# Asking for an expert's down weights one unit later, and summing the late modulation vectors as rows in two free PSUM banks

## The chip, the cores and the metric

The program runs on one core of a Trainium2 chip. Its time is the device time in microseconds (us) of one execution; the median of several executions is compared. All numbers are float32.

## The reference, cut to what matters

The block takes 512 tokens of width 1024. Six modulation vectors come from one vector `c`; then comes a mixer (a chunked state-space branch and a sliding-window attention branch, gated and merged, one output projection, a residual), and then a mixture of 64 experts, of which each token uses 6.

```python
mod = jax.nn.silu(c) @ ada_w[i] + ada_b[i]
sh1, sc1, g1, sh2, sc2, g2 = [m[:, None, :] for m in jnp.split(mod, 6, axis=-1)]
...
merged = gates[:, :, 0] * ssd_branch + gates[:, :, 1] * attn_branch
h = h + g1 * (merged @ w_out[i])
n2 = rms_norm(h, norm2_g[i]) * (1.0 + sc2) + sh2
...
for e in range(N_EXPERTS):
    hid = jax.nn.silu(n @ e_gate[e]) * (n @ e_up[e])
    out = out + (hid @ e_down[e]) * combine[:, e:e + 1]
```

An expert has a gate and an up matrix of 1024 x 256 and a down matrix of 256 x 1024, 1 MiB each, 192 MiB for all 64. `sh2`, `sc2`, `g1` and `g2` are the "late" vectors: they are first needed after the merge.

## The kernel before, in words

Each engine has its own instruction list, written out by hand, and semaphores tie the lists together. SyncE (SP) issues nearly all loads of weights, GpSimd (POOL) the indirect gathers and scatters.

**The merge.** For each of four column blocks `i` TensorE computes three products `b` (gate of branch A, gate of branch B, attention projection) in banks `4 * jj + b` of the eight PSUM banks; `jj` is 0 or 1. So banks 3 and 7 hold nothing then. ScalarE takes the sigmoid of `b` 0 and 1 (`g_sig`), VectorE multiplies and adds (`g_read`, `merged_done`). In the trace all these products stand under line 1635 (L1635): `n1T,ring` is `b` 0 and 1, `attT,ring` is `b` 2.

**The late vectors.** Before the merge VectorE has built four partial sums of 128 partitions x 1024, one for each late vector (`late_acc`, which the trace names `siluz`), and they still have to be summed over the partitions. TensorE does this after block `i == 1`, behind waits for the merge of that block (`g_sig`, `g_read`), since it uses banks 0 to 4: for `g1` and `g2` four matmuls with an all-ones matrix, which give the sum on every partition as a row (L1645), and for `sh2` and `sc2` 16 matmuls of one output column each, which give the sum as a column (L1649). VectorE adds the biases (L1140 to L1145), and TensorE waits for that (`late_read`) before block `i == 2`.

**The experts.** The work is a sequence of units. A unit is 128 gathered rows: of one expert, or 64 each of two. The first 36 units (`BEFORE`) are unrolled, in the order `FPFPFPFP` and then four times `SPSPSSP` (F and S: one expert, P: two); a loop runs the remaining units, two experts each. TensorE does for unit `v`: the gates and ups (`gate_up`, L1771), the transposes of the next unit's rows (L1759), then the downs of unit `v - 1` (`down`, L1779), then the transposes of its own hidden rows (L1786). `gate_up` releases `gu_ready`, `down` releases `ey_ready`.

There are six slots for weights (`gu_*` for gate and up, `dn_*` for down). When a unit has used its slots, SP refills them with the experts of `REFILL[un]`: it reads the experts' numbers (`expert`, L473), waits for the gates and ups of unit `un`, issues the loads of gates and ups (L459, L460), waits for the downs of unit `un`, which TensorE does only behind the gates and ups of unit `un + 1`, issues the loads of downs (L463), and goes to the next unit. All go through one queue. The loop behind the unrolled units has the same order of waits in code of its own.

Of the kernel before, what the change touches and what calls it, by code (L numbers as in the profile page):

```python
# [13 lines left out]
SEQ = 512  # L14
D = 1024
# [74 lines left out]
def hybrid_ssd_swa_moe_adaln_block(nc, a):  # L90
# [36 lines left out]
    OUTER = 6  # L127
    PARTS = [slice(0, 1), slice(1, 3), slice(3, KC)]
    NLATE = 4 * KC

    w_gate = a["exp_w_gate"][0].rearrange("e (p k) f -> e p k f", k=KC)
    w_up = a["exp_w_up"][0].rearrange("e (p k) f -> e p k f", k=KC)
# [7 lines left out]
    with ExitStack() as ctx:  # L140
# [82 lines left out]
        def flat(ap):  # L223
            return ap.rearrange("p a b -> p (a b)")
# [171 lines left out]
        def load_turns(eng):  # L396
            eng.wait_ge(ordered, TABLE)
            return eng.value_load(turns_i[0:1, 0:1], min_val=0, max_val=4) + 1

        @block.sync  # L400
        def _(sp):
# [60 lines left out]
            def load_dn(s, e):  # L462
                sp.dma_start(dn(s)[:, :, :], which(w_down, e)).then_inc(dn_in[s], 16)  # L463
# [16 lines left out]
            load_gu(FIXED + 1, ids[1])  # L480
            sp.wait_ge(sy_ready, T)
            load_dn(FIXED + 1, ids[1])
            for un in range(BEFORE):
                ids = [expert(r) for r in REFILL[un]]
                if ids:
                    sp.wait_ge(gu_ready, un + 1)
                    for r, e in zip(REFILL[un], ids):
                        load_gu(SLOT[r], e)
                    sp.wait_ge(ey_ready, un + 1)
                    for r, e in zip(REFILL[un], ids):  # L490
                        load_dn(SLOT[r], e)
            count = load_turns(sp)
            with sp.Fori(0, count) as j:
                for m in range(LAST):
# [439 lines left out]
        def _(dve):  # L934
            steps = [0]

            def chain(ins):

                steps[0] += 1
                ins.then_inc(dve_step, 1)  # L940
                dve.wait_ge(dve_step, steps[0])
# [179 lines left out]
                    late_step(m)  # L1121
            for m in range(2 * NCH, NLATE):
                late_step(m)
            for i in range(D // WB):
                for jj in range(2):
                    dve.wait_ge(b_done, 2 * i + jj + 1)
                    dve.wait_ge(g_sig, 4 * i + jj + 1)
                    dve.tensor_tensor(sg[jj], branch[2 * i + jj], sg[jj], ALU.mult).then_inc(g_ssd, 1)
                for jj in range(2):
                    dve.wait_ge(g_ready, 6 * i + 4 + jj + 1)  # L1130
                    dve.wait_ge(g_sig, 4 * i + 2 + jj + 1)
                    dve.tensor_tensor(sg[2 + jj], ps[:, 4 * jj + 2, :], sg[2 + jj], ALU.mult).then_inc(g_read, 1)
                    dve.wait_ge(g_ssd, 2 * i + jj + 1)
                    dve.wait_ge(g_read, 2 * i + jj + 1)
                    dve.tensor_tensor(mergedT[:, 2 * i + jj, :], sg[jj], sg[2 + jj], ALU.add).then_inc(merged_done, 1)  # L1135
                if i == 1:

                    dve.wait_ge(late_ready, 1)
                    dve.wait_ge(vec_in, 16 * NVEC)
                    dve.tensor_tensor(g1_row[:, :], g1_row[:, :], flat(ps[:, 0:2, :]), ALU.add)  # L1140
                    dve.tensor_tensor(g2_row[:, :], g2_row[:, :], flat(ps[:, 2:4, :]), ALU.add)
                    dve.tensor_tensor(mod2[:, 1, :], ps[:, 4, 0:8], ab[0], ALU.add)
                    chain(dve.tensor_tensor(mod2[:, 0, :], ps[:, 4, 8:16], ab[1], ALU.add))
                    chain(dve.tensor_scalar(mod2[:, 0, :], mod2[:, 0, :], 1.0, None, ALU.add))
                    dve.tensor_tensor(mod2[:, 0, :], mod2[:, 0, :], n2g, ALU.mult).then_inc(late_read, 1)  # L1145
            dve.wait_ge(late_read, 1)
            dve.wait_ge(x_in[0], 32)

            def residual(t, half):
# [246 lines left out]
        def _(pe):  # L1396
# [224 lines left out]
                    qk(c + 2)  # L1621


            pe.wait_ge(att_done, NCH)
            for i in range(D // WB):
                for b in range(3):
                    w = block_in(BLK_M + 3 * i + b)
                    src = (n1T, n1T, attT)[b]
                    for jj in range(2):
# [5 lines left out]
                            ins = pe.matmul(ps[:, 4 * jj + b, :], w[:, k, P * jj:P * jj + P], src[:, k, :],  # L1635
                                            start=(k == 0), stop=(k == KC - 1))
                        ins.then_inc(g_ready, 1)
                if i == 1:

                    pe.wait_ge(late_used, NLATE)  # L1640
                    pe.wait_ge(g_sig, 8)
                    pe.wait_ge(g_read, 4)
                    for s, bank in ((0, 0), (3, 2)):
                        for half in range(2):
                            pe.matmul(ps[:, bank + half, :], ones[:, :], late_acc[:, s, BANK * half:BANK * half + BANK],  # L1645
                                      start=True, stop=True)
                    for s in range(2):
                        for k in range(KC):
                            ins = pe.matmul(ps[:, 4, 8 * s + k:8 * s + k + 1],  # L1649
                                            late_acc[:, 1 + s, :].rearrange("p (f k) -> p k f", k=KC)[:, k, :],  # L1650
                                            ones[:, 0:1], start=True, stop=True)
                    ins.then_inc(late_ready, 1)
                    pe.wait_ge(late_read, 1)
            pe.wait_ge(g_sig, 16)
            pe.wait_ge(g_read, 8)
            pe.wait_ge(merged_done, KC)

            def out_rows(t, b):
                w = block_in(BLK_OUT + b)
# [252 lines left out]
```

## Time and profile before

| what | value |
|---|---|
| time of the kernel before, median of 3 | 1306.63 us (1306.05 to 1307.37) |
| time of the profiled execution | 1308.78 us |
| its span, from the first to the last instruction | 1307.1 us |
| TensorE (PE) busy | 1200.8 us, 92% |
| VectorE (DVE), ScalarE (ACT), GpSimd (POOL) busy | 36%, 19%, 15% |
| mean granted TensorE clock | 0.971 |
| moved by the DMA engines | 322.29 MB |

PE busy, DVE busy and so on are shares of the span. The granted clock is the share of TensorE's full 2.4 GHz clock that it was given; it has two levels, 1.00 (2.4 GHz) and 0.50 (1.2 GHz). "DMA share" is the mean busy share of the core's 16 DMA engines; since packets overlap a little it can read 1.01 or 1.02. A name such as `SPq` is the queue of instructions of an engine, in which it waits and issues transfers. In the names of the trace `_lo` and `_hi` are two parts of the six slots.

### The profile page before, as it was taken

Reading aid. Unit: us, or ns where it says so; the run is one execution under the profiler, and the core shown is the slowest. Engines: PE = TensorE matmul, PEld = TensorE weight load, DVE = VectorE, ACT = ScalarE, POOL = GpSimd, SP = SyncE. Lnnn points to the kernel's source line nnn. Section 1 sums busy time; section 2 is a strip of 40 time slices with the busy share of each in tenths; the row PEclk is TensorE's granted clock in tenths of the full one; section 3 lists DMA queues with packets and bytes.
Section 4 is the critical chain, followed back from the end, with each engine's and each line's share of the span. In section 5 each row is a group of like instructions: output and inputs, shape, how many; then the busy total and the mean of one; then the engine's idle time right before and its main releaser. Section 6 shows DMA issues by size and latency. Waiting matters only on the chain. (4 is left out here: it accounts for less than half of the span.)

```text
span 1307.1 us, 13433 instructions
## 1 busy us (share of the span) xinstructions
PE 1200.8 (92%) x4827; PEld 621.5 (48%) x4827; DVE 473.3 (36%) x986; ACT 246.0 (19%) x611; POOL 195.8 (15%) x320
## 2 busy tenths in 40 slices
PE   4999999998999999999999999989989989988866
PEld 2536864465554444448854444434434434433322
DVE  4685034665566101113765232222323222222225
ACT  2141122234441000001121121111212111111101
POOL 4000021111012000010261212212121212211100
PEclk9999999999999998999999999989989999999988
DMA  9642241213548141237157899999999999999646
GB/s 301 186 129 64 78 149 65 97 33 129 160 125 296 65 161 33 65 105 322 72 198 274 301 419 422 423 424 421 417 396 419 400 388 412 353 414 412 264 196 276
DMA packets 108106, 322.29 MB, mean 247 GB/s; under 512 B 14500, under 2 KB 67832, under 8 KB 81032
## 3 DMA queue, kind: packets, MB, share of 16 engines
q1 hardware_dynamic: 87824, 269.37, 53.8%
q0 software_dynamic: 18688, 47.30, 10.1%
q10 hardware_dynamic: 1528, 4.77, 0.9%
q8 instruction: 39, 0.64, 0.2%
q14 instruction: 27, 0.22, 0.0%
HBM read 314.49 MB, written 26.82 MB: 261 GB/s over the span
## 5 line engine op out<-in xcount | busy, mean ns | idle before, releaser
L1771 PE MATMUL ps<-gu_hi,xsT 128*64 128x512 f32 (+1 forms) x704 | 247.5, 622 | 27.1 <-issue 14.3
L1771 PE MATMUL ps<-gu_lo,xsT 128*64 128x512 f32 (+1 forms) x320 | 152.3, 632 | 12.6 <-DMA gu_hi<-in_exp_w_up_dram 6.7
L1771 PEld LDWEIGHTS ps<-gu_hi,xsT 128*64 128x64 f32 (+1 forms) x704 | 86.3, 156 | 137.4 <-issue 135.1
L1308 DVE SCALAR_TENSOR_TENSOR hid<-ps,wgt,gated 128x256 f32<-128x256 f32 x42 | 20.3, 484 | 313.1 <-ACT gated L908 313.1
L1779 PE MATMUL ps<-dn_hi,hidT 128*64 128x512 f32 (+1 forms) x352 | 119.9, 597 | 1.1 <-DVE hn L1304 1.1
L1635 PE MATMUL ps<-n1T,ring 128*128 128x512 f32 x256 | 112.3, 600 | 3.7 <-DVE mod L1145 3.0
L1415 PE MATMUL ps<-n1T,ring 128*128 128x512 f32 x256 | 111.9, 594 | 0.0
L683 POOL DMA_INDIRECT expert_rows<-hn,meta x42 | 41.9, 998 | 416.7 <-DVE hn L1304 374.6
L1304 DVE TENSOR_TENSOR hn<-ps,g_row 128x1024 f32<-128x1024 f32 x42 | 51.4, 1225 | 94.7 <-PE ps L1779 94.7
L1771 PEld LDWEIGHTS ps<-gu_lo,xsT 128*64 128x64 f32 (+1 forms) x320 | 52.6, 170 | 66.7 <-issue 65.5
L1635 PEld LDWEIGHTS ps<-n1T,ring 128*128 128x128 f32 x256 | 49.2, 193 | 65.0 <-issue 61.1
L908 ACT ACTIVATE gated<-ps 128x256 f32<-128x256 f32 x42 | 16.1, 383 | 339.4 <-PE ps L1771 339.4
L1415 PEld LDWEIGHTS ps<-n1T,ring 128*128 128x128 f32 x256 | 48.2, 190 | 58.6 <-issue 58.6
L1779 PE MATMUL ps<-dn_lo,hidT 128*64 128x512 f32 (+1 forms) x160 | 72.5, 596 | 0.0
L1423 PE MATMUL ps<-ring,n1T 128*128 128x256 f32 x320 | 71.1, 383 | 0.0
L898 ACT ACTIVATE xsT<-ps,mod 128x128 f32<-128x128 f32 x172 | 64.6, 456 | 26.7 <-PE ps L1759 26.7
L1423 PEld LDWEIGHTS ps<-ring,n1T 128*128 128x128 f32 x320 | 61.3, 193 | 9.2 <-issue 1.2
L1779 PEld LDWEIGHTS ps<-dn_hi,hidT 128*64 128x64 f32 (+1 forms) x352 | 38.7, 150 | 48.1 <-issue 46.2
L1298 DVE TENSOR_SCALAR xsT<-ps,mod 128x128 f32<-128x128 f32 x172 | 58.8, 404 | 5.4 <-PE ps L1759 5.4
L1608 PE MATMUL ps<-xbcT,ring 128*128 128x512 f32 x128 | 58.4, 599 | 0.0
L1663 PE MATMUL ps<-ring,raw 128*128 128x256 f32 x256 | 56.6, 380 | 1.8 <-DVE raw L1135 1.8
L1759 PEld LDWEIGHTS ps<-ident,hn 128*128 128x128 f32 x344 | 42.9, 191 | 29.3 <-issue 27.5
(333 smaller groups left out, 1345.4 us busy)
## 6 DMA issues: line engine op xcount, KB each, us to landing
gu_hi<-in_exp_w_gate_dram SPq DMA_DIRECT2D x44, 1024.0 KB, 16.5
gu_hi<-in_exp_w_up_dram SPq DMA_DIRECT2D x44, 1024.0 KB, 29.7
dn_hi<-in_exp_w_down_dram SPq DMA_DIRECT2D x44, 1024.0 KB
ring<-in_w_in_dram SPq DMA_DIRECT2D x21, 1024.0 KB, 5.6
gu_lo<-in_exp_w_gate_dram SPq DMA_DIRECT2D x20, 1024.0 KB
gu_lo<-in_exp_w_up_dram SPq DMA_DIRECT2D x20, 1024.0 KB
dn_lo<-in_exp_w_down_dram SPq DMA_DIRECT2D x20, 1024.0 KB
h<-in_ada_w_dram POOLq DMA_DIRECT2D x32, 512.0 KB, 4.9
```

The costliest lines, as they stand in the source:

```text
L683: pool.indirect_dma_start(out=rows_d[:, :], out_offset=bass.IndirectOffsetOnAxis(ap=meta[:, c, 1:2], axis=0), in_=ys[:, b, :], in_offset=N ...
L898: ins = act.activation(xsT[:, b, k, :], ps[:, 0, P * k:P * k + P], ACT.Identity, bias=B2[:, k:k + 1], scale=A2[:, k:k + 1])
L1298: ins = dve.tensor_scalar(xsT[:, b, k, :], ps[:, 1, P * (k - 4):P * (k - 4) + P], A2[:, k:k + 1], B2[:, k:k + 1], ALU.mult, ALU.add)
L1304: dve.tensor_tensor(ys[:, b, :], flat(ps[:, 5:7, :]), g2_row[:, :], ALU.mult).then_inc(ey_dve, 1)
L1415: ins = pe.matmul(bank, w[:, k, lo:lo + P], n1T[:, k, :], start=(k == 0), stop=(k == KC - 1))
L1423: ins = pe.matmul(bank[:, 0:WB], n1T[:, k, P * t:P * t + P], w[:, k, :], start=(k == 0), stop=(k == KC - 1))
L1608: ins = pe.matmul(ps[:, 1, :], w[:, k, P * (m % 2):P * (m % 2) + P], uT[:, k, :], start=(k == 0), stop=(k == KC - 1))
L1635: ins = pe.matmul(ps[:, 4 * jj + b, :], w[:, k, P * jj:P * jj + P], src[:, k, :], start=(k == 0), stop=(k == KC - 1))
L1663: ins = pe.matmul(ps[:, 2 * (t % 2) + b // 2, WB * (b % 2):WB * (b % 2) + WB], mergedT[:, k, P * t:P * t + P], w[:, k, :], start=(k == 0), ...
L1759: ins = pe.transpose(ps[:, k // 4, P * (k % 4):P * (k % 4) + P], xs[:, b, :].rearrange("p (f k) -> p k f", k=KC)[:, k, :], ident[:, :])
L1771: ins = pe.matmul(ps[rows, 2 + b, :], xsT[:, b, k, rows], gu(s)[:, :, k, :], start=(k == 0), stop=(k == KC - 1))
L1779: ins = pe.matmul(ps[rows, 5 + half, :], hidT[:, jj, rows], dn(s)[:, jj, BANK * half:BANK * half + BANK], start=(jj == 0), stop=(jj == 1))
```

## The change

**Downs one unit later.** In the unrolled units SP now keeps the downs of a unit in the list `downs`, and issues them after the gates and ups of the next unit. The wait for `gu_ready` of the next unit therefore stands ahead of the wait for `ey_ready`, and is reached earlier. The loop is as before.

**Late vectors.** All four are summed as rows (`late_sum`), two matmuls of 512 columns each, in banks 3 and 7, at four places of the merge (`LATE_AT`), in the order `sh2, sc2, g1, g2` (`LATE_ORDER`). The 16 matmuls of one column are gone, and so are the waits for `g_sig` and `g_read`. On VectorE `late_out` adds the two row vectors to their biases; for `sh2` and `sc2` it multiplies the row with the identity matrix, so that each partition keeps its own eight values (`diagonal`), and reduces that to a column.

```diff
@@ constants @@
+    LATE_ORDER = (1, 2, 0, 3)
+    LATE_AT = ((0, 2), (1, 0), (1, 2), (2, 0))
@@ SyncE, unrolled units @@
+            downs = []
             for un in range(BEFORE):
                 ids = [expert(r) for r in REFILL[un]]
                 if ids:
                     sp.wait_ge(gu_ready, un + 1)
                     for r, e in zip(REFILL[un], ids):
                         load_gu(SLOT[r], e)
-                    sp.wait_ge(ey_ready, un + 1)
-                    for r, e in zip(REFILL[un], ids):
+                if downs:
+                    sp.wait_ge(ey_ready, un)
+                    for r, e in downs:
                         load_dn(SLOT[r], e)
+                downs = list(zip(REFILL[un], ids))
@@ VectorE, merge @@
+            diagonal = work[:, 4 * SEQ:4 * SEQ + D]
+            def late_out(n):
+                s = LATE_ORDER[n]
+                dve.wait_ge(late_ready, n + 1)
+                if n == 0:
+                    dve.wait_ge(vec_in, 16 * NVEC)
+                for half in range(2):
+                    bank, cols = ps[:, 3 + 4 * half, :], slice(BANK * half, BANK * half + BANK)
+                    if s in (0, 3):
+                        row = (g1_row, g2_row)[s // 3][:, cols]
+                        ins = dve.tensor_tensor(row, row, bank, ALU.add)
+                    else:
+                        ins = dve.tensor_tensor(diagonal[:, cols].rearrange("p (f k) -> p f k", k=KC),
+                                                bank.rearrange("p (f k) -> p f k", k=KC),
+                                                over(ident[:, HALF * half:HALF * half + HALF], KC), ALU.mult)
+                ins.then_inc(late_read, 1)
+                if s in (0, 3):
+                    return
+                dve.wait_ge(late_read, n + 1)
+                col = mod2[:, 2 - s, :]
+                chain(dve.tensor_reduce(col, diagonal.rearrange("p (f k) -> p k f", k=KC), AX.X, ALU.add))
+                chain(dve.tensor_tensor(col, col, ab[s - 1], ALU.add))
+                if s == 2:
+                    chain(dve.tensor_scalar(col, col, 1.0, None, ALU.add))
+                    chain(dve.tensor_tensor(col, col, n2g, ALU.mult))
...
+                if (i, 0) in LATE_AT:
+                    late_out(LATE_AT.index((i, 0)))
...
-                if i == 1:
-                    dve.wait_ge(late_ready, 1)
-                    dve.wait_ge(vec_in, 16 * NVEC)
-                    dve.tensor_tensor(g1_row[:, :], g1_row[:, :], flat(ps[:, 0:2, :]), ALU.add)
-                    dve.tensor_tensor(g2_row[:, :], g2_row[:, :], flat(ps[:, 2:4, :]), ALU.add)
-                    dve.tensor_tensor(mod2[:, 1, :], ps[:, 4, 0:8], ab[0], ALU.add)
-                    chain(dve.tensor_tensor(mod2[:, 0, :], ps[:, 4, 8:16], ab[1], ALU.add))
-                    chain(dve.tensor_scalar(mod2[:, 0, :], mod2[:, 0, :], 1.0, None, ALU.add))
-                    dve.tensor_tensor(mod2[:, 0, :], mod2[:, 0, :], n2g, ALU.mult).then_inc(late_read, 1)
+                if (i, 2) in LATE_AT:
+                    late_out(LATE_AT.index((i, 2)))
@@ TensorE, merge @@
+            def late_sum(n):
+                pe.wait_ge(late_used, NLATE)
+                if n >= 1:
+                    pe.wait_ge(late_read, n)
+                for half in range(2):
+                    ins = pe.matmul(ps[:, 3 + 4 * half, :], ones[:, :],
+                                    late_acc[:, LATE_ORDER[n], BANK * half:BANK * half + BANK], start=True, stop=True)
+                ins.then_inc(late_ready, 1)
...
-                if i == 1:
-                    pe.wait_ge(late_used, NLATE)
-                    pe.wait_ge(g_sig, 8)
-                    pe.wait_ge(g_read, 4)
...
-                    ins.then_inc(late_ready, 1)
-                    pe.wait_ge(late_read, 1)
+                    if (i, b) in LATE_AT:
+                        late_sum(LATE_AT.index((i, b)))
...
+            pe.wait_ge(late_read, len(LATE_ORDER))
```

How the change moves TensorE's instructions in the merge. Before, from block `i == 0` to the start of block `i == 3` (L1635 the products, L1645 the row sums, L1649 the column sums):

```order
L1635 MATMUL ps<-attT,ring 128x512 x16
L1635 MATMUL ps<-n1T,ring 128x512 x32
L1635 MATMUL ps<-attT,ring 128x512 x16
L1645 MATMUL ps<-siluz,ones 128x512 x4
L1649 MATMUL ps<-ones,siluz 128x1 x16
L1635 MATMUL ps<-n1T,ring 128x512 x32
```

Of the changed kernel, the same stretch (L1672 the products, L1657 the sums):

```order
L1672 MATMUL ps<-attT,ring 128x512 x16
L1657 MATMUL ps<-siluz,ones 128x512 x2
L1672 MATMUL ps<-n1T,ring 128x512 x16
L1657 MATMUL ps<-siluz,ones 128x512 x2
L1672 MATMUL ps<-n1T,ring 128x512 x16
L1672 MATMUL ps<-attT,ring 128x512 x16
L1657 MATMUL ps<-siluz,ones 128x512 x2
L1672 MATMUL ps<-n1T,ring 128x512 x16
L1657 MATMUL ps<-siluz,ones 128x512 x2
```

The 20 matmuls behind block 1 have become four pairs, each behind a run of products that doesn't touch banks 3 and 7.

How it moves SP's loads behind unit 0. Before, from the refill after unit 0 to that after unit 2 (`TENSOR_LOAD order` reads an expert's number):

```order
L459 DMA gu_hi<-in_exp_w_gate_dram 128x2048
L460 DMA gu_hi<-in_exp_w_up_dram 128x2048
L463 DMA dn_hi<-in_exp_w_down_dram 128x2048
L473 TENSOR_LOAD order
L473 ISA x2
L473 TENSOR_LOAD order
L473 ISA x2
L459 ISA
L459 DMA gu_hi<-in_exp_w_gate_dram 128x2048
L460 DMA gu_hi<-in_exp_w_up_dram 128x2048
```

Of the changed kernel, from the same refill on:

```order
L461 DMA gu_hi<-in_exp_w_gate_dram 128x2048
L462 DMA gu_hi<-in_exp_w_up_dram 128x2048
L475 TENSOR_LOAD order
L475 ISA x2
L475 TENSOR_LOAD order
L475 ISA x2
L461 ISA
L461 DMA gu_hi<-in_exp_w_gate_dram 128x2048
L462 DMA gu_hi<-in_exp_w_up_dram 128x2048
L461 ISA
L461 DMA gu_hi<-in_exp_w_gate_dram 128x2048
L462 DMA gu_hi<-in_exp_w_up_dram 128x2048
```

The down of the refill behind unit 0, which stood between the two groups of gates and ups, now comes behind the second, as the next row of the list:

```order
L465 DMA dn_hi<-in_exp_w_down_dram 128x2048
```

## Rows read from the trace of the kernel before

**Rows 1.** The page, the span in 40 slices of 32.7 us: DMA.

```profile
DMA  9642241213548141237157899999999999999646
GB/s 301 186 129 64 78 149 65 97 33 129 160 125 296 65 161 33 65 105 322 72 198 274 301 419 422 423 424 421 417 396 419 400 388 412 353 414 412 264 196 276
```

**Rows 2.** The chain that ended last, two of its transfers: start, us, what.

```profile
1079.35 35.08 DMA gu_lo<-in_exp_w_up_dram
...
1208.07 27.62 DMA gu_lo<-in_exp_w_up_dram
```

**Rows 3.** What PE waited for from 860 to 1240: total, times, longest.

```profile
PE ps L1771 <- issue: 19.2, 9, 4.2
PE ps L1771 <- DMA gu_hi<-in_exp_w_up_dram: 13.8, 6, 4.5
PE ps L1771 <- DMA gu_lo<-in_exp_w_up_dram: 4.9, 3, 3.5
```

**Rows 4.** PE's timeline in the merge: start, us, line, operands, [idle before].

```profile
442.60 27.63 PE L1635 MATMUL ps<-n1T,ring 128*128 128x512 f32 x64
470.07 13.90 PE L1635 MATMUL ps<-attT,ring 128*128 128x512 f32 x32
484.84 3.67 PE L1645 MATMUL ps<-siluz,ones 128*128 128x512 f32 x8 [0.88 <-DVE work L1132]
488.35 7.53 PE L1649 MATMUL ps<-ones,siluz 128*128 128x1 f32 x32
498.88 29.28 PE L1635 MATMUL ps<-n1T,ring 128*128 128x512 f32 x64 [3.00 <-DVE mod L1145]
527.99 13.90 PE L1635 MATMUL ps<-attT,ring 128*128 128x512 f32 x32
```

**Rows 5.** Windows: stretch, us, busy of PE, PEld, DVE, ACT, POOL, then PEclk, DMA share, GB/s.

```profile
492.00:499.00 7.00, 4.00 (x18) 3.91 (x17) 2.84 (x6) 0.00 (x0) 0.00 (x0) 0.50 0.00 0
499.00:502.00 3.00, 3.00 (x4) 1.38 (x5) 0.00 (x0) 0.00 (x0) 0.00 (x0) 0.50 0.03 5
```

**Rows 6.** DVE's timeline in the merge, and its reductions of 1024 elements.

```profile
477.13 0.69 DVE L1132 TENSOR_TENSOR work<-ps,work 128x512 f32<-128x512 f32 x1 [19.21 <-PE ps L1635]
...
L1090 DVE TENSOR_REDUCE mx<-seg x8: 686/1220/1220, 308.1 to 382.6; 128x8 f32<-128x1024 f32 x7, 128x8 f32<-128x512 f32 x1
```

**Rows 7.** SP's timeline behind the first units.

```profile
721.98 0.33 SPq L463 DMA_DIRECT2D dn_hi<-in_exp_w_down_dram  x1
723.63 0.33 SPq L459 DMA_DIRECT2D gu_hi<-in_exp_w_gate_dram  x1
...
733.55 0.81 SPq L463 DMA_DIRECT2D dn_hi<-in_exp_w_down_dram  x2
735.11 0.33 SPq L459 DMA_DIRECT2D gu_hi<-in_exp_w_gate_dram  x1
```

**Rows 8.** PE's timeline: gates and ups of units 1 and 2.

```profile
710.34 7.09 PE L1771 MATMUL ps<-gu_hi,xsT 128*64 128x512 f32 x32 [1.18 <-ACT xsT L898]
...
722.01 7.03 PE L1771 MATMUL ps<-gu_hi,xsT 128*128 128x512 f32 x16
```

**Rows 9.** Windows of the experts' stage, columns as in rows 5.

```profile
717.50:722.50 5.00, 5.00 (x20) 2.85 (x21) 2.36 (x6) 2.13 (x6) 0.00 (x0) 1.00 0.00 0
722.50:735.00 12.50, 12.26 (x46) 5.42 (x46) 4.18 (x11) 2.37 (x7) 3.80 (x6) 1.00 0.98 361
735.00:750.00 15.00, 15.00 (x58) 6.91 (x55) 3.33 (x9) 2.27 (x6) 3.77 (x7) 1.00 1.02 312
750.00:940.00 190.00, 181.69 (x684) 80.08 (x683) 49.32 (x120) 34.03 (x90) 36.45 (x61) 0.98 1.02 422
940.00:1110.00 170.00, 158.62 (x594) 70.75 (x593) 42.90 (x105) 29.88 (x79) 30.73 (x52) 0.97 0.99 403
1110.00:1140.00 30.00, 27.56 (x91) 13.09 (x89) 9.67 (x24) 6.42 (x17) 4.92 (x9) 1.00 0.92 350
```

**Rows 10.** Loads of ups (L460) issued from 1040 to 1240.

```profile
DMA to landing us min/median/max: 27.7/29.0/30.8
```

More of the change, by code:

```diff
@@ L1135, in _ @@
                     dve.tensor_tensor(mergedT[:, 2 * i + jj, :], sg[jj], sg[2 + jj], ALU.add).then_inc(merged_done, 1)
-                if i == 1:
-                    dve.wait_ge(late_ready, 1)
-                    dve.wait_ge(vec_in, 16 * NVEC)
-                    dve.tensor_tensor(g1_row[:, :], g1_row[:, :], flat(ps[:, 0:2, :]), ALU.add)
-                    dve.tensor_tensor(g2_row[:, :], g2_row[:, :], flat(ps[:, 2:4, :]), ALU.add)
-                    dve.tensor_tensor(mod2[:, 1, :], ps[:, 4, 0:8], ab[0], ALU.add)
-                    chain(dve.tensor_tensor(mod2[:, 0, :], ps[:, 4, 8:16], ab[1], ALU.add))
-                    chain(dve.tensor_scalar(mod2[:, 0, :], mod2[:, 0, :], 1.0, None, ALU.add))
-                    dve.tensor_tensor(mod2[:, 0, :], mod2[:, 0, :], n2g, ALU.mult).then_inc(late_read, 1)
-            dve.wait_ge(late_read, 1)
+                if (i, 2) in LATE_AT:
+                    late_out(LATE_AT.index((i, 2)))
+            dve.wait_ge(late_read, len(LATE_ORDER))
             dve.wait_ge(x_in[0], 32)
@@ L1637, in _ @@
                         ins.then_inc(g_ready, 1)
-                if i == 1:
-                    pe.wait_ge(late_used, NLATE)
-                    pe.wait_ge(g_sig, 8)
-                    pe.wait_ge(g_read, 4)
[L1643 to L1651, printed above, removed]
-                    ins.then_inc(late_ready, 1)
-                    pe.wait_ge(late_read, 1)
+                    if (i, b) in LATE_AT:
+                        late_sum(LATE_AT.index((i, b)))
             pe.wait_ge(g_sig, 16)
```

## The prediction, made before the changed kernel ran

> **What bounds the kernel now.** I read the slices of the page first, for whether the transfers or TensorE set the pace. From the 24th slice to the 37th the DMA line reads 9 and the rate is about 420 GB/s, with dips to 388 and 353 [rows 1]. So the experts' stage moves weights as fast as this core does anywhere in the trace. The chain of waits says the same: its long pieces are loads of ups, on the way for 35.1 and 27.6 us [rows 2], and from 860 us on TensorE waits 19.2 + 13.8 + 4.9 = 37.9 us in front of its gates and ups [rows 3]. Before the experts the mean rate is mostly under 200 GB/s [rows 1], and there I read TensorE's timeline for gaps. In the merge it has one place with waits and with matmuls of one column [rows 4].
>
> So the two halves of the change meet two limits. The late vectors stand on TensorE's own path, where a microsecond saved moves everything behind it, the start of the experts' loads too, since these wait for TensorE's events. The order of the loads acts in a stage that the DMA queue limits. There nothing is won by asking early, unless the queue stood empty.
>
> **Part 1, the late vectors.** Step one, what the block costs now. Ends of matmuls overlap, so I count from start to start: the 32 products of `n1T` take 470.07 - 442.60 = 27.47 us, and by the same pace the 16 of `attT` take half of it, 13.73 us [rows 4]. From the start of `attT` in block 1 (470.07) to the start of `attT` in block 2 (527.99) stand 16 + 32 products, worth 13.73 + 27.47 = 41.20 us. It took 57.92 us. The block of sums therefore costs 16.72 us: 488.35 - 483.80 = 4.55 us for the four row sums with the gap ahead (0.88 of it a wait for VectorE), 7.53 us for the 16 column sums, 3.00 us of wait for VectorE's biases, and 29.11 - 27.47 = 1.64 us in the products behind it (29.11 being 527.99 - 498.88).
>
> The 1.64 us have a reason that a row shows: the granted clock was 0.50, the lower level of 1.2 GHz, from 492 to 502 us, while TensorE did the matmuls of one column and then waited [rows 5]; the products that began at 498.88 ran their first three microseconds at that level. If I left this out, the block would cost 15.08 us. The Trainium skill (TensorE: Matmul & The Clock Gate, What's actually happening) says that the low clock is the default and that activity releases it, and the trace agrees, with its 0.50 behind the thin matmuls and the wait. By that rule the dense sums of the changed kernel keep the clock up.
>
> Step two, what it costs after. Four matmuls of 512 columns took 488.35 - 484.84 = 3.51 us [rows 4], so eight take 7.0 us. The bounds: 6.9 us at the pace of the products (27.47 / 32 = 0.86 each), and 10.5 us if each of the four pairs has a wait of 0.88 us of its own ahead of it. I take 7.0, the nearest row. The gain is 16.7 - 7.0 = 9.7 us, between 6.2 and 9.8.
>
> Step three, the new waits. TensorE's `late_sum(n)` waits for VectorE's `late_out(n - 1)`. At least one run of 16 products, 13.73 us, lies between two sums, and two runs ahead of the third. `late_out` with a reduction is two operations of 128 x 512 out of PSUM (0.69 each), a reduction of 1.22 us and two or four tiny ones: about 3 us [rows 6]; even at double price it is 6 us. VectorE had been idle for 19.21 us when it took up block 1's attention products at 477.13 [rows 6], so its new work lies in idle time, and the merge behind it (`g_read`) is not late. I cost all of it at nothing; without that cover it would be 2 x 3 + 2 x 1.4, about 9 us in all.
>
> Step four, does it reach the end? The merge, the output projection and the routing follow from TensorE's merge, and the first loads of experts are released by it. I count the 9.7 us in full.
>
> **Part 2, downs one unit later.** The gates and ups of unit 1 end at 710.34 + 7.09 = 717.43, which is `gu_ready` for the refill behind it. SP asked for that refill's gates and ups only at 723.63, because it stood in the wait for the downs of unit 0 (issued at 721.98) [rows 7, 8]. And from 717.5 to 722.5 the DMA engines moved nothing at all [rows 9]. After the change the 4 MiB of unit 1's refill are asked for at about 717.6, so the engines start 721.98 - 717.6 = 4.4 us earlier. The bounds: nothing, if they run empty again soon, and 723.63 - 717.6 = 6.0 us, how much earlier the gates are asked for.
>
> Does the queue then run empty later on? In the changed order 5.2 MB (the 4 MiB and the down) are asked for by 722. At 361 to 422 GB/s they last 12.4 to 14.5 us from about 719, to 731 or later; unit 2's gates and ups end at 722.01 + 7.03 = 729.04, and then the next 2 MiB are asked for, six microseconds ahead of the 735.11 of before [rows 7 to 9]. So it stays filled, and the 4.4 us are kept. From 722.5 on it is filled before as well: the share is 0.98 or more up to 940 [rows 9].
>
> What of the dips behind 940? The shares 0.99 and 0.92 and the rates 403 and 350 against 422 [rows 9] look like time in which the queue was short of requests, and the change asks for gates some 6 us earlier in each of these units too. Against this stands one row: no load of ups from 1040 on landed sooner than 27.7 us after it was asked for [rows 10], while 2 MiB at 422 GB/s take 5 us. With such a tail of requests a mean share below one can't mean that all 16 engines had run out. Some had and some were behind, and a transfer has landed only when the last engine has done its part. I take it that the slowest engines never ran empty from 722 on, and that their work sets the landings. Asking earlier gives work to those that can only wait. I cost these dips at nothing. The Trainium skill (DMA: Bandwidth & Descriptors, Why a DMA increments its semaphore by 16 and not by 1) says that the engines of a transfer finish independently and that only the full count means landed. No row of mine shows single engines; by this rule the gain of part 2 is the 4.4 us, by the mean share it would be that of the rival below.
>
> The order itself brings TensorE a unit's gates ahead of the last unit's downs, so it waits less in the middle. But the last loads, in the loop, are in the old order, and what lies ahead of them is the same number of bytes.
>
> **Sum.** 9.7 + 4.4 = 14.1 us. The profiled execution of before took 1308.78 us with a span of 1307.1, 0.16% above the median; I expect a span of 1293.0, and take the same off the median: 1306.6 - 14.1 = 1292.5 us.
>
> **Rivals.**
> - *Only part 1 pays* (13 in 100): the earlier start is eaten before the queue first holds TensorE up, for instance because the lists and the gather, at 312 GB/s from 735 to 750 [rows 9], come to lie against more traffic. For it: that stretch has small packets. Against it: they are a fixed amount of work. 1306.6 - 9.7 = 1296.9 us.
> - *The mean rate counts* (12 in 100): the queue was short of requests in truth. Then 940 to 1110 would run at 422, worth 170 x (1 - 403 / 422) = 7.7 us, and of 1110 to 1140, where the loop's old order begins, up to 30 x (1 - 350 / 422) = 5.1 us [rows 9]. 1292.5 - 7.7 - 5.1 = 1279.7 us, and 1284.8 with the first alone.
> - *The downs come late* (4 in 100), the one that ends slower. Place: TensorE in front of L1779. A unit's downs now have the next unit's gates and ups ahead of them, 2 or 4 MiB, 5 to 10 us at 422 GB/s. Of the 42 units' downs each can wait. It decides only when these waits outgrow what TensorE now waits for gates, 37.9 us [rows 3], plus the gain of 14.1: over 52 / 42 = 1.2 us for each. With 3 us each, 126 - 52 = 74 us is lost, about 1380; with 1.5 us each 11 us, about 1318. Against it: in the queue the new order is the order of use, gates of `v`, then downs of `v - 1`; a single expert's downs then land 2.5 us behind the gates, and TensorE needs 7 us for these.
> - *It doesn't do what it says* (3 in 100): VectorE takes up the sums late and TensorE waits at each as long as it did, and part 2 as in the first rival. About 1306.
>
> **How the numbers follow.** My forecast has 68 in 100, by itself 1291 to 1296: up by the 3.5 us of waits in part 1, down by the 1.6 us between 4.4 and 6.0. The range reaches up to the case of part 1 alone with its lower gain, 1306.6 - 6.2 = 1300.4, and down to where the mean rate counts for half of its 12.8 us, 1286.1: 1286 to 1300. About 0.2% (2.6 us) is what a measurement of this kernel can tell from no change. Faster by more: all but the last two rivals, 0.93; within it 0.03; slower 0.04.
>
> **What the changed profile would show.** Part 1 right: no matmul of one column, no wait for VectorE between blocks 1 and 2, the clock 1.00 through the merge, and 41.2 + 3.5 = 44.7 us from the `attT` of block 1 to that of block 2, where two of the four pairs stand (57.92 before). Part 2 right: no window without traffic behind unit 1, the first gates after it asked for right behind unit 1's; the stretch from the first unit's gates to the last unit's 4.4 us shorter; TensorE's waits smaller in the middle, and still there in the loop; loads of ups still some 28 us on the way. The mean rate rival would show as 420 GB/s from 940 to 1110 together with an end of the loads over 10 us earlier relative to unit 0. I would be wrong most of all if the dips are idle time of all engines, or if a gather that comes late holds the units up.

## The result, and the profile after

The changed kernel takes 1292.13 us (median of 4 runs, 1291.88 to 1294.68); the kernel before, on the same chip in between, 1307.0 us (4 runs, 1306.05 to 1308.8). The ratio of the two is 0.988, with a 95% interval of 0.9864 to 0.9896. The span of the profiled execution is 1290.4 us with a mean granted clock of 0.981 (before 1307.1 and 0.971). The prediction was 1292.5 us.

The DMA slices of the page of the changed kernel [answers to rows 1]:

```profile
DMA  9742242213449232337256999999999999999647
GB/s 300 192 131 65 66 137 93 90 42 131 131 131 307 84 130 66 96 104 315 93 204 265 346 421 421 423 423 421 413 409 410 395 400 403 377 388 421 268 189 289
```

TensorE's timeline of the changed kernel, in the merge, at units 1 and 2, and at the first unit of the loop (L1672 the products, L1657 the sums, L1795 gates and ups) [rows 4, 8]:

```profile
427.34 13.90 PE L1672 MATMUL ps<-attT,ring 128*128 128x512 f32 x32
441.07 1.88 PE L1657 MATMUL ps<-siluz,ones 128*128 128x512 f32 x4
442.79 13.90 PE L1672 MATMUL ps<-n1T,ring 128*128 128x512 f32 x32
...
471.98 13.90 PE L1672 MATMUL ps<-attT,ring 128*128 128x512 f32 x32
485.71 1.88 PE L1657 MATMUL ps<-siluz,ones 128*128 128x512 f32 x4
487.43 13.90 PE L1672 MATMUL ps<-n1T,ring 128*128 128x512 f32 x32
501.16 1.88 PE L1657 MATMUL ps<-siluz,ones 128*128 128x512 f32 x4
502.88 13.90 PE L1672 MATMUL ps<-n1T,ring 128*128 128x512 f32 x32
516.61 13.90 PE L1672 MATMUL ps<-attT,ring 128*128 128x512 f32 x32
...
698.83 7.09 PE L1795 MATMUL ps<-gu_hi,xsT 128*64 128x512 f32 x32 [1.19 <-ACT xsT L903]
...
710.51 7.03 PE L1795 MATMUL ps<-gu_hi,xsT 128*128 128x512 f32 x16
...
1140.67 9.40 PE L1795 MATMUL ps<-gu_hi,xsT 128*64 128x512 f32 x32 [8.63 <-DMA gu_hi<-in_exp_w_up_dram]
```

The four pairs take 1.72 us each, from start to start, and nothing waits between them. From `attT` of block 1 to `attT` of block 2 it is 516.61 - 471.98 = 44.63 us, where it was 57.92. The wait of 8.63 us in the last row is new.

VectorE's timeline at the first sum (L1143 the product with the identity, L1151 the reduction) and at the next block's attention products [rows 6]:

```profile
442.99 1.29 DVE L1143 TENSOR_TENSOR work<-ps,ident 128x512 f32<-128x512 f32 x2 [0.23 <-PE ps L1657]
444.31 2.01 DVE L1151 TENSOR_REDUCE mod<-work 128x8 f32<-128x1024 f32 x1
446.36 0.17 DVE L1152 TENSOR_TENSOR mod<-mod,vec 128x8 f32<-128x8 f32 x1
...
479.10 0.69 DVE L1167 TENSOR_TENSOR work<-ps,work 128x512 f32<-128x512 f32 x1 [16.73 <-PE ps L1672]
```

SP's timeline behind unit 1 [rows 7]; L461 and L462 are gates and ups, L465 downs:

```profile
706.09 0.33 SPq L461 DMA_DIRECT2D gu_hi<-in_exp_w_gate_dram  x1
...
707.51 0.53 SPq L462 DMA_DIRECT2D gu_hi<-in_exp_w_up_dram  x1
710.47 0.33 SPq L465 DMA_DIRECT2D dn_hi<-in_exp_w_down_dram  x1
717.71 0.33 SPq L461 DMA_DIRECT2D gu_hi<-in_exp_w_gate_dram  x1
```

Windows of the changed kernel, columns as in rows 5: the merge, then the stretches of [rows 9], each 11.5 us earlier; the last row is from the first gates of unit 1 to the first of the last unit:

```profile
492.00:499.00 7.00, 7.00 (x17) 3.04 (x16) 0.69 (x1) 0.60 (x1) 0.00 (x0) 1.00 0.01 2
...
706.00:711.00 5.00, 5.00 (x20) 2.85 (x21) 2.37 (x6) 2.13 (x6) 0.00 (x0) 1.00 0.77 279
711.00:723.50 12.50, 12.50 (x48) 5.49 (x48) 4.18 (x11) 2.37 (x7) 3.80 (x6) 1.00 1.03 357
723.50:738.50 15.00, 15.00 (x57) 6.55 (x54) 3.33 (x9) 2.27 (x6) 4.08 (x8) 1.00 1.02 316
738.50:928.50 190.00, 184.65 (x712) 81.22 (x712) 52.18 (x126) 36.40 (x96) 36.15 (x61) 1.00 1.01 421
928.50:1098.50 170.00, 155.82 (x581) 71.20 (x580) 43.20 (x107) 29.56 (x78) 30.74 (x52) 0.99 1.01 404
1098.50:1128.50 30.00, 30.00 (x114) 13.57 (x113) 7.13 (x18) 5.02 (x14) 7.09 (x12) 1.00 0.96 377
...
698.83:1220.74 521.91, 480.12 (x1857) 211.04 (x1857) 131.61 (x320) 91.00 (x241) 95.51 (x160) 0.98 0.99 397
```

The same stretch of the kernel before:

```profile
710.34:1236.18 525.84, 486.28 (x1856) 213.36 (x1857) 131.55 (x320) 90.76 (x241) 95.73 (x161) 0.97 0.97 394
```

This pair of rows is worth a look. The stage is 525.84 - 521.91 = 3.93 us shorter. The product of length and rate is the same 207.2 MB in both, so the stage lasts as long as its bytes. And TensorE's idle time did not fall, it is 39.6 us before and 41.8 us after: what fell is its busy time, by 6.2 us, while the granted clock was lower less often (0.98 and 0.97 before, 1.00 and 0.99 after in the two long stretches). This split is not the change's doing. Two kernels of the next section, `downs_only` and then `first_down_only`, have the same length of the stage with more busy time, less idle time and a lower clock:

```profile
708.88:1230.73 521.85, 485.02 (x1857) 212.67 (x1857) 131.50 (x320) 91.00 (x241) 95.50 (x160) 0.97 0.98 397
...
700.66:1223.10 522.44, 487.59 (x1856) 213.38 (x1857) 131.51 (x320) 91.01 (x241) 94.69 (x159) 0.97 0.98 397
```

So TensorE spends the shortage of weights partly as waits (34.9 to 41.8 us) and partly as slower work (480.1 to 487.6 us busy), in shares that differ between executions, and the length does not follow them.

What TensorE waited for in the changed kernel from 850 to 1225 us [rows 3]:

```profile
PE ps L1795 <- issue: 15.8, 7, 2.9
PE ps L1795 <- DMA gu_hi<-in_exp_w_up_dram: 15.2, 5, 8.6
PE ps L1795 <- DMA gu_lo<-in_exp_w_up_dram: 7.7, 3, 4.3
```

The view of [rows 10] gives no landing for the ups of this execution, because it leaves out the slots of which the trace lacks a semaphore event. The events themselves give it: one comes from each DMA engine for each transfer, so a load of gates and ups has landed with the last of its 32 (2 of the 18 loads lack one). Counted so, the 18 loads of ups issued from 1040 to 1240 landed 25.8 to 32.3 us after they were asked for, 30.1 at the median.

### The profile page after: what moved, and what is told of

Same layout as the page of the kernel before. It is cut to its first block and busy times, and to the rows that moved or that the text cites. A ratio compares the mean times of both kernels' runs of the same rounds, so it can differ in the third digit from the quotient of the medians.

```text
span 1290.4 us, 13395 instructions
## 1 busy us (share of the span) xinstructions
PE 1187.4 (92%) x4803; PEld 611.3 (47%) x4803; DVE 480.3 (37%) x994; ACT 246.4 (19%) x611; POOL 196.2 (15%) x320
## 5 line engine op out<-in xcount | busy, mean ns | idle before, releaser
L1795 PE MATMUL ps<-gu_hi,xsT 128*64 128x512 f32 (+1 forms) x704 | 241.8, 614 | 30.1 <-DMA gu_hi<-in_exp_w_up_dram 11.6
L1795 PE MATMUL ps<-gu_lo,xsT 128*64 128x512 f32 (+1 forms) x320 | 145.8, 609 | 9.8 <-issue 6.0
L1795 PEld LDWEIGHTS ps<-gu_hi,xsT 128*64 128x64 f32 (+1 forms) x704 | 84.6, 155 | 140.2 <-issue 138.6
L1672 PE MATMUL ps<-n1T,ring 128*128 128x512 f32 x256 | 110.9, 592 | 0.7 <-ACT attT L857 0.7
L1331 DVE TENSOR_TENSOR hn<-ps,g_row 128x1024 f32<-128x1024 f32 x42 | 51.4, 1225 | 95.2 <-PE ps L1803 95.2
L1795 PEld LDWEIGHTS ps<-gu_lo,xsT 128*64 128x64 f32 (+1 forms) x320 | 51.1, 165 | 60.3 <-issue 59.8
L1672 PEld LDWEIGHTS ps<-n1T,ring 128*128 128x128 f32 x256 | 48.6, 190 | 61.6 <-issue 60.7
L1635 PE MATMUL ps<-xbcT,ring 128*128 128x512 f32 x128 | 58.4, 599 | 0.0
```

Of the source, the lines that this page charges most:

```text
L1331: dve.tensor_tensor(ys[:, b, :], flat(ps[:, 5:7, :]), g2_row[:, :], ALU.mult).then_inc(ey_dve, 1)
L1635: ins = pe.matmul(ps[:, 1, :], w[:, k, P * (m % 2):P * (m % 2) + P], uT[:, k, :], start=(k == 0), stop=(k == KC - 1))
L1795: ins = pe.matmul(ps[rows, 2 + b, :], xsT[:, b, k, rows], gu(s)[:, :, k, :], start=(k == 0), stop=(k == KC - 1))
```

## The experiments

One table first, since most verdicts rest on it. Each kernel's time is given with its ratio to the kernel before, which ran beside it, and the 95% interval of this ratio. The kernel before had medians of 1307.0 to 1308.3 us in these groups of runs, so between groups ratios compare better than medians. For each kernel the table has the median and, read from TensorE's timeline, the start of block 0's `attT`, the merge (from there to block 3's `attT`) and the experts (from unit 1's gates to the last unit's). The start moves between 427.0 and 430.0 us although the code ahead of it is the same in all, so single spans differ by that much for no reason of an edit; the two lengths are free of it. The experts' length has a scatter of its own: it is 521.85, 521.91 and 522.56 us in three kernels with the new order of loads, 525.84 and 527.07 in two with the old one. So I read nothing from 1 us of it. "n" is the number of timed runs.

```
kernel                 median   n   start   merge    experts
before                 1307.0   4   428.87  140.32   525.84
changed                1292.13  4   427.34  130.47   521.91
sums_only              1297.54  5   427.25  130.47   527.07
downs_only             1305.24 11   427.52  140.28   521.85
first_down_only        1292.28  5   429.11  130.46   522.44
all_but_first_down     1296.12  4   429.62  130.47   525.85
ask_late               1291.81  5   427.01  130.47   523.53
thin_in_free_bank      1302.85 10   428.70  139.04   522.56
rows_in_place          1297.12  6   429.37  130.46   524.88
rows_spread            1306.93 12   428.53  130.46   534.30
lists_early            1286.62  5   429.05  130.47   514.82
upper_shifted          1293.55  5   429.97  130.47   520.77
shifted_and_early      1285.84  5   426.96  130.46   514.68
```

### Each part alone

`sums_only` has SP's old order, `downs_only` the old late sums.

```diff
@@ sums_only, against the changed kernel @@
-                if downs:
-                    sp.wait_ge(ey_ready, un)
-                    for r, e in downs:
+                    sp.wait_ge(ey_ready, un + 1)
+                    for r, e in zip(REFILL[un], ids):
```

> The late vectors as in the changed kernel, the downs in the order of before. If part 1 is worth what the timelines of before and after show from block 0 to block 3 of the merge (9.8 us) and part 2 the rest, 1297.2 us against 1307.0 of the kernel before (ratio 0.9925). If the first part's gain were partly given back later and the loads' order did more, above 1299; if the sums gave all of it, 1292.

> The downs as in the changed kernel, the late vectors as before. My theory: the request queue's empty stretch behind unit 1 is filled, 4 us and no more: 1303.0 us against 1307.0 (ratio 0.997). The rival by which the mean rate of the queue counts: 8 to 12 us, 1295 to 1299. If the two parts only pay together: 1307.

Measured: `sums_only` 1297.54 us (ratio 0.9919, 0.9906 to 0.9933), `downs_only` 1305.24 us (0.9974, 0.9964 to 0.9985). In the table each part moves one length: the sums the merge, 140.32 to 130.47, and the downs the experts, 525.84 to 521.85; the 1.2 us by which the experts of `sums_only` are longer than before is within the scatter. They add up: 9.85 + 3.99 = 13.84 us. The median of `downs_only` shows less of it, 2 to 5 us by its interval.

### Which refill pays

`first_down_only` postpones only the down of unit 0's refill; `all_but_first_down` postpones all others.

```diff
@@ behind downs = list(zip(REFILL[un], ids)); the second kernel has un >= 1 @@
+                if not (un == 0) and downs:
+                    sp.wait_ge(ey_ready, un + 1)
+                    for r, e in downs:
+                        load_dn(SLOT[r], e)
+                    downs = []
```

> As the changed kernel, but only the down of the first refill is asked for behind the next unit's gates; all later refills are in the order of before. My theory: the whole gain of part 2 lies in that first place, since only there the queue was empty: the time of the changed kernel, 1292 to 1293 us. The rival, that asking 6 us earlier helps at each of the 32 refills: most of part 2 is lost, 1296 us.

> As the changed kernel, but the first refill's down is asked for at once, as before, and all later ones behind the next unit's gates. My theory: the empty stretch behind unit 1 is back, and the later requests only meet a long queue: about 1296 us, 4 us above the changed kernel. The rival, many small gains: 1292 to 1293.

Measured: 1292.28 us (0.9884, 0.9863 to 0.9906) and 1296.12 us (0.9906, 0.9891 to 0.9921). One transfer postponed gives the whole gain of part 2. The downs of the 31 other refills give nothing by the table (525.85 against 525.84), and 1.4 us by the medians (1296.12 against 1297.54 of `sums_only`).

### Asking later from unit 10 on

```diff
+                    if un >= 10:
+                        sp.wait_ge(ey_ready, un + 1)
```

This stands ahead of the gates and ups, whose downs then follow at once.

> As the changed kernel up to unit 9; from unit 10 on SP asks for gates and ups only when the downs of the same unit are done, some 12 us later than the changed kernel, and for the downs right behind. My theory: with loads of ups some 25 to 30 us on the way, the slowest DMA engines don't run empty by it: 1292 to 1294 us. The rival, that the mean rate below 422 GB/s is a shortage of requests: asking 12 us later makes the shortage several times larger, 1300 us or more.

Measured: 1291.81 us (0.9879, 0.9859 to 0.9899); the experts are 1.6 us longer than in the changed kernel, little more than the scatter. In the traces, counted from unit 1, the gates and ups of units 10 and later are asked for 9 to 19 us later up to 1095 us, and their last semaphore events come 0 to 7 us later there and under 2 us later from 1104 us on. So in a queue that is behind anyway, the moment of asking is worth next to nothing, even in the direction that should hurt.

### Thin matmuls without their wait

`sh2` and `sc2` are summed by eight one-column matmuls each, as before the change, but in the free bank 3 and at the changed kernel's places, so that nothing waits for them.

```diff
+                    for k in range(KC):
+                        ins = pe.matmul(ps[:, 3, k:k + 1],
+                                        late_acc[:, LATE_ORDER[n], :].rearrange("p (f k) -> p k f", k=KC)[:, k, :],
+                                        ones[:, 0:1], start=True, stop=True)
```

> As the changed kernel, but sh2 and sc2 are summed by eight matmuls of one column each, in bank 3 at the same two places, and VectorE has no diagonal to form. It tells the price of the thin matmuls from that of the waits. By the trace of before, eight cost 7.53 / 2 = 3.8 us, in place of 1.75 us for two of 512 columns: 4 us over the changed kernel, about 1296. If the low clock follows the thin matmuls alone, without a wait: up to 1.6 us more at each place, 1298 to 1299. If the waits were all that cost: 1292.

Measured: 1302.85 us (0.996, 0.9946 to 0.9974), 10.7 us more than the changed kernel. TensorE's timeline of this kernel, and two of its windows:

```profile
442.43 3.73 PE L1657 MATMUL ps<-ones,siluz 128*128 128x1 f32 x16
446.02 15.68 PE L1673 MATMUL ps<-n1T,ring 128*128 128x512 f32 x32
461.54 3.73 PE L1657 MATMUL ps<-ones,siluz 128*128 128x1 f32 x16
465.13 16.94 PE L1673 MATMUL ps<-n1T,ring 128*128 128x512 f32 x32
481.91 13.90 PE L1673 MATMUL ps<-attT,ring 128*128 128x512 f32 x32
```

```profile
443.00:450.00 7.00, 7.00 (x20) 4.67 (x20) 1.19 (x3) 0.00 (x0) 0.00 (x0) 0.80 0.48 150
...
460.00:470.00 10.00, 10.00 (x26) 6.46 (x26) 1.20 (x4) 0.60 (x1) 0.00 (x0) 0.71 0.34 106
```

No wait stands in these rows, and yet the products behind the thin matmuls take 15.52 and 16.78 us from start to start, not 13.73. The granted clock was 0.80 and 0.71 of full on average in the two windows, so part of each ran at the lower of its two levels. The bill: 2 x (3.59 - 1.72) = 3.7 us for the thin matmuls themselves and 1.79 + 3.05 = 4.8 us for the clock behind them, together the 8.57 us by which the merge is longer. The profiled spans are 10.1 us apart; 1.4 us of what is left is the later start. The Trainium skill (TensorE: Matmul & The Clock Gate, What's actually happening) makes activity the thing that holds the clock up. In these rows TensorE shows as busy without a gap and lost the clock all the same, so gaps in its busy time do not account for this case.

### Why the 16 engines drift apart

My prediction had taken it that single engines are behind. The semaphore increments in the trace, one per engine and transfer, show it. This is my own count of them (before, then the changed kernel):

```
before   gu0 first 711.9   last 716.1  of 32 increments
before   gu0 first 759.6   last 766.1
changed  gu4 first 951.3   last 980.3  (29.0 us apart)
changed  gu3 first 1200.9  last 1220.4, dn1 last 1222.9, dn3 last 1225.8
```

The 32 increments of such a pair are those of two transfers, so a part of the 29 us is the second one. The 16 increments of a single down, asked for at 940.9, go from 948.3 to 973.5 us: by then the last engine is some 25 us behind the first. The last increments follow each other without a gap, 2.4 to 3.7 us for a down and 4.8 to 7.3 for a pair of gates and ups, to the end of the loads. I read from this that the fast engines run empty, which is the share below 1, and that the slow ones set the landings. `ask_late` fits: there the increments of a down lie at most 18.3 us apart, the fast engines being asked later, and the last ones of the gates and ups hardly move. `rows_spread` puts place 8x+y of a unit's list of tokens on partition 8y+x, to spread the rows of gathers and scatters over the engines; it needs eight small list transfers per half, and `rows_in_place` is its control, with these transfers and the old places.

```diff
+        def read_list(eng, half, y, blocks):
+            rows = slice(HALF * half + 8 * y, HALF * half + 8 * y + 8)
+            return eng.dma_start(lists[rows, 0:EMPTY, :].rearrange("p (b e) w -> p b (e w)", b=NBLK)[:, blocks, :],
+                                 list_d.rearrange("(b x y e) w -> y x b (e w)", b=NBLK, x=8, y=8)[y][:, blocks, :])
```

> As the changed kernel, but the lists of tokens are read so that list place 8x + y stands on partition 8y + x of its half, so gathers and scatters of a unit that isn't full have their rows spread over all partitions instead of the first ones. The read takes 8 small transfers for each half. If the slowest DMA engines are those that serve the first partitions, whose rows are there in each unit, they lose a third of their work for gathers and scatters, some 30 us: the loads land sooner, TensorE's 38 us of waits mostly go, and the time is 1260 to 1275 us. If the engines differ for another reason, nothing changes: 1292 to 1296 us.

> The control of rows_spread: the same small transfers for the lists, but each row on the partition where the changed kernel has it. By both theories the time of the changed kernel or a little more: 1291 to 1296 us.

Measured: 1306.93 us (0.9989, 0.9979 to 0.9999) and 1297.12 us (0.9915, 0.99 to 0.9931). My theory, eight partitions in a row to an engine, fell: the spread made it 9.8 us slower than its control. That the places matter is shown, since only the order of the rows differs. In its trace 12 engines ran ahead and 4 trailed (of a down asked for at 955.9 us the 12th increment comes after 18.7 us, the last four after 29.1 to 30.9), which would fit row q on engine q mod 16. `upper_shifted` tests that.

```diff
+            ups = [(lists[HALF + SHIFT:P, 0:EMPTY, :], slice(0, HALF - SHIFT)),
+                   (lists[HALF:HALF + SHIFT, 0:EMPTY, :], slice(HALF - SHIFT, HALF))]
```

> The changed kernel, with the list places of the upper half moved by 10 partitions against those of the lower half, so that other DMA engines serve the empty places. Theory (row q of a gather or scatter goes to engine q mod 16; an engine moves about 26.7 KB/us and a row is 8 KiB): the fullest engine now has 217 of 3072 rows where the mean is 192, 7.7 us more than its share; with the shift 205, 4.0 us more. So 3.7 us less: about 1288.4 us, and the distance between the first and the last engine of a load, 26 to 29 us, falls by a third or more. Rival (the engines drift apart for another reason): 1291 to 1293 and the same distance.

Measured: 1293.55 us (0.9883, 0.9862 to 0.9905), and the first and the last increment are 29.7 us apart at the pair that had 29.0. The second theory missed too. Other assignments were not tried, so how rows fall to engines stays open.

### The lists' transfer in an emptier queue

The dip to 316 GB/s from 723.5 to 738.5 us was left over from the kernel before [rows 9]. There POOL asks for the rest of the routing lists, two transfers of 384 KB, behind unit 2's transposes. `lists_early` asks for them ahead of unit 0.

```diff
+            pool.wait_ge(sy_ready, T)
+            pool.dma_start(lo[:, 2:, :], list_v[:, 2:, :]).then_inc(lists_rest, 16)
+            pool.dma_start(hi[:, 2:, :], list_v[:, 2:, :]).then_inc(lists_rest, 16)
             for un in range(BEFORE):
...
-                if un == 2:
-                    pool.wait_ge(sy_ready, T)
-                    pool.dma_start(lo[:, 2:, :], list_v[:, 2:, :]).then_inc(lists_rest, 16)
-                    pool.dma_start(hi[:, 2:, :], list_v[:, 2:, :]).then_inc(lists_rest, 16)
```

> The changed kernel, with the transfer of the large rest of the lists asked for by POOL before the first unit, right behind the shared expert's input, instead of behind the transposes of unit 2. In the changed kernel the core moves 316 GB/s from 723.5 to 738.5 us, where that transfer of many small pieces runs, against 421 behind it. Theory (rate counts wherever the queue is full, and small pieces cost it): in the emptier queue before 707 us the transfer costs nothing, and 15 x (1 - 316/422) = 3.8 us come back: 1288.4 us, at most twice that, 1285. Rival (the 316 is the gather's and the scatter's doing, or the transfer costs as much wherever it stands): no change, 1291 to 1293.

> Both edits together. If both theories hold, the sum: 1284 to 1285 us. If one holds, 1288 to 1289; if neither, 1291 to 1293.

Measured: `lists_early` 1286.62 us (1285.96 to 1287.03, ratio 0.9832, 0.9813 to 0.985), `shifted_and_early` 1285.84 us (0.9834, 0.9813 to 0.9855). Windows of `lists_early`, columns as before:

```profile
706.00:711.00 5.00, 5.00 (x22) 2.49 (x19) 1.85 (x5) 1.89 (x5) 0.00 (x0) 1.00 0.48 152
711.00:723.50 12.50, 12.50 (x45) 5.56 (x43) 3.28 (x8) 2.27 (x6) 2.36 (x4) 1.00 1.01 414
723.50:738.50 15.00, 15.00 (x61) 6.57 (x60) 4.75 (x11) 2.65 (x7) 3.05 (x5) 1.00 1.02 409
...
700.56:1215.38 514.82, 483.25 (x1856) 211.06 (x1857) 131.60 (x320) 90.78 (x241) 93.78 (x158) 0.98 0.99 401
```

The dip is gone, 316 became 409 and 357 became 414, and the experts are 7.1 us shorter. By time the gain over the changed kernel is 5.5 us, which is 0.4%; the two intervals do not touch (0.985 and 0.9864). It is above the 3.8 us expected; the stretch ahead of the dip gained as well. 768 KB at 422 GB/s would be 1.9 us: in a full queue these transfers cost about three times what their bytes do. The trace also shows the other loads slowed: from 723 to 737 us of the changed kernel a packet of 8192 bytes takes 341 to 509 ns, averaged over stretches of 2 us, against 309 to 317 ns up to 719 us and 309 to 385 ns in `lists_early` from 722 to 738. By the kernel's access pattern the pieces of the lists are 1 KiB, though the trace records them in packets of 4096 bytes. That the small pieces are the reason is likely but not shown, since no run changes the size of the pieces alone. `lists_early` and `shifted_and_early` are the fastest kernels of the study, and both are told apart from the changed one. The shift added to the early lists gave nothing that can be measured.

## Why the prediction was right

**What bounds the kernel.** Both limits held. The merge's saving went to the end in full: from block 3's `attT` to unit 1's gates it is 141.15 us before and 141.02 after.

**Part 1, step one and two.** Forecast 9.7 us; the merge is 9.85 us shorter. The dense sums kept the clock at 1.00 from 492 to 499 us, where it was 0.50. The distance of 44.63 us against 44.7 forecast says that no pair had a wait. The term of 1.64 us for the clock was right in kind. I had put it down to thin matmuls and a wait together; `thin_in_free_bank` shows that no wait is needed, and that two groups of thin matmuls with products behind each cost more, 4.8 us.

**Part 1, step three.** `late_out` was mis-sized. Its reduction reads with a stride and took 2.01 us, where I had taken 1.22 from contiguous ones, so that it takes 3.5 us for the first vector and 3.9 for the second, not 3. It stayed hidden, as said: VectorE was still idle for 16.73 us ahead of block 1's attention products.

**Part 2.** Forecast 4.4 us; the experts are 3.93 us shorter, 3.99 in `downs_only` against before, and 5.16 against `sums_only`. The window without traffic is gone (279 GB/s where there was 0), and `first_down_only` shows that this is where all of it comes from. That the rest of the reordering is worth nothing, or 1.4 us at most, the step that I was least sure of, is shown by `all_but_first_down` and `ask_late`. The rival of the mean rate fell with them: from 928.5 to 1098.5 the rate is 404 against 403 [rows 9], although the gates are asked for earlier.

**Where I was wrong in detail.** I forecast smaller waits in the middle and the same in the loop. Waits from 850 us on are 38.7 us, against 37.9 [rows 3]; they begin later (the first of over 2 us for weights at 904 us, not 869) and one of 8.63 us appears at the loop's first unit. Neither the waits nor the clock tells where the 3.93 us came back, since their shares differ between executions of equal length. Loads of ups were 30.1 us on the way at the median, close to the 28 that I had said. My reading of [rows 10] was too strong, though: the view covers 6 of the 20 loads of ups of that stretch, and by the semaphore events the soonest landed after 25.5 us, not 27.7, with a median of 29.4. The argument needs only that they were far above 5 us. And of the stretch with 312 GB/s I said that lists and gathers are "a fixed amount of work"; true of the bytes, but `lists_early` shows that their price depends on the place.

**The sum.** 9.85 + 3.93 = 13.8 us against 14.1. The medians are 14.9 us apart and the profiled spans 16.7, of which 1.5 is the start of the merge, on which the change has no part, and 1.3 the tail; the profiled execution of before was the longest of its four, and the prediction had put it 0.16% above the median. That the forecast of 1292.5 us lies 0.4 us from the 1292.13 measured is in part luck: against the 1307.0 us that the kernel before took this time, the same sum gives 1292.9, and the medians of the kernel before moved by 1.3 us between groups of runs.

**Left open.** Why the engines drift apart by some 25 us, why the lists' transfer costs more than its bytes, how the rows of gathers and scatters fall to engines, and why the start of the merge moves by up to 3 us between executions.

## What to carry to other kernels

In a stage that moves a fixed number of bytes through a full queue, reordering requests pays only where the queue stands empty, so look for windows with a rate of zero and fix those alone; then look for a dip in the rate inside the full stretch, and ask for the transfer that lies there where the queue is not full. Sum over partitions with wide matmuls in a free bank rather than with one-column ones: the thin form took twice as long here (3.59 us against 1.72 for one vector), and lowered the clock for the dense work behind it. Measure lengths between fixed instructions of a trace, not only spans, since the latter carried up to 3 us that no edit had caused, and learn the scatter of such a length from kernels that are the same in it.

## What the runs showed of the hardware

- One-column float32 matmuls in a row, with no gap in TensorE's busy time, went with a granted clock of 0.80 and 0.71 on average over 7 and 10 us, and the dense matmuls behind them took 1.8 and 3.1 us longer (`thin_in_free_bank`).
- Under weight loads mixed with gathers and scatters the 16 DMA engines drift up to 25 us apart within one transfer of 1 MiB. Asking for gates and ups 9 to 19 us later moved the experts' length by 1.6 us (`ask_late`).
- 768 KB of lists cost 5.5 us of the kernel's time in a full queue, 1.9 us by their bytes. The Trainium skill (DMA: Bandwidth & Descriptors, Why small descriptors are slow) has some 3 cycles per packet beside 32 bytes a cycle, which for pieces of 1 KiB is an estimate of 9% more, 2.0 us; the measurement is far above it, and may have other causes than the pieces.
- Lists read by eight transfers of eight partitions for each half instead of one, the later ones spread over eight units, cost 5 us (1297.12 against 1292.13 us). The dip from 723.5 to 738.5 us is gone there (407 GB/s), and the long stretch behind it runs at 406 GB/s instead of 421.
